# Products of zeros on TensorE, in a two-block transformer on one Trainium2 core

## The reference

```python
h = x * rsqrt(mean(x**2, -1) + eps) * norm_g * (1 + scale) + shift   # second block
x = x + 0.5 * gate[0] * swiglu(h, w_in, w_out)                       # feed-forward
x = x + gate[1] * mixer(adaln(x))
```

## Time and profile before

| | |
|---|---|
| median of 3 runs | 3921.24 us (3918.16 to 3923.84) |
| profiled execution | 3914.14 us, span 3912.5 us |
| mean granted clock of TensorE | 0.905 of 2.4 GHz |
| TensorE busy (matmul) | 3438.6 us, 88% of the span |
| VectorE busy | 2347.7 us, 60% |
| ScalarE busy | 1507.4 us, 39% |

### The profile page before, as it was taken

The page is one execution under the profiler, slowest core; times in us unless marked ns, Lnnn a source line. Parts: engine busy times, 40 slices in busy tenths (PEclk is TensorE's granted clock), DMA queues, the critical chain, the costliest instruction groups (busy, mean ns, idle before and its releaser), DMA issues. The chain is left out here.

```text
span 3912.5 us, 68263 instructions
## 1 busy us (share of the span) xinstructions
PE 3438.6 (88%) x28885; PEld 3248.8 (83%) x28885; DVE 2347.7 (60%) x3355; ACT 1507.4 (39%) x2038; POOL 155.0 (4%) x148
## 2 busy tenths in 40 slices
PE   6688999999985788999997499999599999859799
PEld 5578999999983778999995499999389998648599
DVE  5547886456764436767676557676657646354454
ACT  3314444434452114444462244444454444311243
POOL 0001111110000100000000000000000000001000
PEclk9769999998997888999996699999799999878799
DMA  8326885445831004768541047685037444200142
GB/s 338 130 119 245 314 311 228 182 187 225 313 135 54 2 2 180 299 235 310 213 172 46 1 186 297 231 310 202 35 153 297 188 185 159 77 21 2 75 175 84
DMA packets 74781, 676.76 MB, mean 173 GB/s; under 512 B 8480, under 2 KB 12608, under 8 KB 52160
## 3 DMA queue, kind: packets, MB, share of 16 engines
q1 hardware_dynamic: 30400, 509.96, 33.6%
q10 hardware_dynamic: 41472, 151.01, 10.1%
q0 software_dynamic: 2688, 12.59, 1.2%
HBM read 669.29 MB, written 4.23 MB: 172 GB/s over the span
## 5 line engine op out<-in xcount | busy, mean ns | idle before, releaser
L1109 DVE TENSOR_TENSOR w_split<-ring,w_split 128x1024 fp32r<-128x1024 f32 x705 | 873.5, 1242 | 603.5 <-ACT w_split L1004 601.1
L1004 ACT ACTIVATE w_split<-ring 128x1024 fp32r<-128x1024 f32 x705 | 742.8, 1057 | 1077.2 <-PE banks L934 853.5
L932 PE MATMUL banks<-u_split,w_split 128*128 128x256 f32 x3840 | 1093.1, 285 | 13.9 <-DVE w_split L1109 7.3
L933 PE MATMUL banks<-u_split,w_split 128*128 128x256 f32 x3840 | 1090.1, 284 | 0.0
L934 PE MATMUL banks<-u_split,w_split 128*128 128x256 f32 x3840 | 1089.9, 284 | 0.0
L932 PEld LDWEIGHTS banks<-u_split,w_split 128*128 128x128 f32 x3840 | 741.5, 193 | 19.8 <-DVE w_split L1109 16.2
L933 PEld LDWEIGHTS banks<-u_split,w_split 128*128 128x128 f32 x3840 | 741.2, 193 | 0.5
L934 PEld LDWEIGHTS banks<-u_split,w_split 128*128 128x128 f32 x3840 | 740.7, 193 | 0.0
L932 PE MATMUL banks<-h_split,w_split 128*128 128x256 f32 x1920 | 543.6, 283 | 2.9 <-DVE w_split L1109 2.9
L933 PE MATMUL banks<-h_split,w_split 128*128 128x256 f32 x1920 | 543.4, 283 | 0.0
L934 PE MATMUL banks<-h_split,w_split 128*128 128x256 f32 x1920 | 543.3, 283 | 0.0
(11 more groups left out here) (395 smaller groups left out, 3986.8 us busy)
## 6 DMA issues: line engine op xcount, KB each, us to landing
ring<-stream SPq DMA_DIRECT2D x147, 3072.0 KB, 10.8
bufs<-ada ACTq DMA_DIRECT2D x288, 512.0 KB, 10.9
bufs<-ada SPq DMA_DIRECT2D x8, 2048.0 KB, 9.0
bufs<-ada POOLq DMA_DIRECT2D x8, 1024.0 KB, 7.6
bufs<-c_rows SPq DMA_DIRECT2D x8, 512.0 KB, 4.3
bufs<-gate_rows POOLq DMA_DIRECT2D x32, 128.0 KB, 8.0
ring<-stream SPq DMA_DIRECT2D x3, 1024.0 KB, 4.9
ring<-stream SPq DMA_DIRECT2D x1, 2816.0 KB, 10.4
```

Source lines behind the costliest of these rows:

```text
L932: pe.matmul(out, w(0), x(0), start=start, stop=False, skip_group_check=True)
L933: pe.matmul(out, w(0), x(1), start=False, stop=False, skip_group_check=True)
L1004: nc.scalar.activation(w_split[:, slot, 0, :], piece(j, b), ACT.Copy).then_inc(high.sem, 1)
L1109: e = nc.vector.tensor_tensor(w_split[:, slot, 1, :], piece(j, b), w_split[:, slot, 0, :].bitcast(F32), ALU.subtract)
```

## The change

`project_first_pair` does its product of zeros ten times instead of once. A new helper, `zero_products`, does `n` products of zeros of 256 columns that add to the right half of a PSUM bank which nobody reads then. `token_sums` gets a parameter `filled`: so many of these products ahead of each chunk's wait. Both kinds of `NextNorm` call it with 1. The root kind also does six of them ahead of the wait for the inverse root, and four behind the spread. The direct calls of `token_sums` in other stages keep `filled=0`.

```diff
@@ project_first_pair
-    pe.matmul(bank, core.zeros[:, 0:P], core.zeros[:], start=True, stop=True)
+    for _ in range(10):
+        pe.matmul(bank, core.zeros[:, 0:P], core.zeros[:], start=True, stop=True)
     pe.wait_ge(low.sem, low.at(2))
@@
+def zero_products(core, pe, bank, n):
+
+    for _ in range(n):
+        pe.matmul(core.psum[:, bank, SEQ:2 * SEQ], core.zeros[:, 0:P], core.zeros[:, 0:SEQ], start=False, stop=True, skip_group_check=True)
+
+
-def token_sums(core, pe, rows, bank, arrived, summed, n=KC, per=1, first=0):
+def token_sums(core, pe, rows, bank, arrived, summed, n=KC, per=1, first=0, filled=0):
     for c in range(first, first + n):
         if arrived and c % per == 0:
+            zero_products(core, pe, (bank + 2) % 8, filled)
             pe.wait_ge(arrived.sem, arrived.at(c // per + 1))
@@ NextNorm.on_tensor, kind "mean"
-            token_sums(core, pe, core.x, self.bank, self.ready, self.summed)
+            token_sums(core, pe, core.x, self.bank, self.ready, self.summed, filled=1)
@@ NextNorm.on_tensor, kind "root"
-            token_sums(core, pe, self.squares, self.bank, self.squared, self.summed)
+            token_sums(core, pe, self.squares, self.bank, self.squared, self.summed, filled=1)
+            zero_products(core, pe, (self.bank + 2) % 8, 6)
             pe.wait_ge(inverse.sem, inverse.at(self.turn + 1))
             spread_tokens(core, pe, 2, ROOT_BANK, self.spread)
+            zero_products(core, pe, (self.bank + 2) % 8, 4)
```

## The result

The changed kernel takes 3939.52 us (median of 5, 3936.33 to 3941.90), the kernel before 3921.24 beside it. The ratio is 1.0050, 95% interval 1.0039 to 1.0061: slower by 18.3 us, where +22.6 was forecast.

The account below looks back on a forecast made before the run. The prediction took TensorE to bound the kernel, in the norms' sums too. Norms +31.1 us less starts 8.5 made +22.6 on the median of 3921.2, so 3944 us; range 3930 to 3952, chance 0.57.

Parts of the forecast that it names:

- The bound of the norms: In the norms' sums TensorE never waits, so each of eight zero products costs its slot: 1.1 us per root norm.
- The 0.5 taken off for a warmer start: Twelfth root norm, before the first macaron stage: 3.0 us at half clock, less 0.5 for a warmer start behind it.
- The eleven: Root norms that follow a dense stage: 2.2 us more each, 24.2 in all.
- The slot of a zero product between one-column ones: In the norms' sums, a 256-column zero product costs 0.12 us at full clock, 0.21 at half; no row showed it.
- The six: Between a root norm's sums and spread: 0 at full clock, 0.45 us at half, taken as 0.3.
- The four: Behind a root norm's spread, with nothing to cover them: 0.48 to 0.85 us, taken as 0.8.
- The mean norms: Three norms: those at 240 and 260 at half clock, 1.7 us each, the one at 865 at full, 1.0; together 4.4.
- The clock falls as now: In the norms the fill is too thin to hold the clock, which falls as before, somewhat later in a few.
- the first rival: The fill holds the clock everywhere, with clock 1.0 throughout the sums: -14 us, 3907; chance 0.12.
- The starts: Ten zero products fill the waits before real products, and the feed-forward starts gain too: 8.5 us back in all.
- Gain 1.3 each, 3.9: Three output stages of 8 chunks: ten zeros fit the 4.61 us wait and real products then run at full clock.
- The signs: In norms: sums 4.6 to 5.5 us, gap near 0.7, next stage 0.5 to 0.9 later, spreads 0.5; output starts clock 1.0.

Follow-up runs that it names:

- e3: Changed kernel with only the eight zero products among the sums of the 15 norms, first pairs with one; 3929.79 us, ratio 1.0032 to the kernel before.
- e5: Changed kernel with only the six zero products ahead of the wait for the inverse root, first pairs with one; 3918.62 us, ratio 1.0002 to the kernel before.
- e4: Changed kernel with only the four zero products behind the spread of the 12 root norms, first pairs with one; 3927.74 us, ratio 1.0024 to the kernel before.
- e9: Changed kernel, norms filled, with the first pairs' zero products in two groups instead of ten in a row; 3931.72 us, ratio 1.0029 to the kernel before.
- e2: Changed kernel with only the fill of the norms, first pairs with one zero product as before; 3943.22 us, ratio 1.0060 to the kernel before.
- e6: Changed kernel with three zero products ahead of each chunk of the sums instead of one; 3949.75 us, ratio 1.0085 to the kernel before.
- e1: Changed kernel with only the ten zero products in front of the first pairs, norms as before; 3904.59 us, ratio 0.9963 to the kernel before.
- e12: The kernel of e1 run again on another day; 3904.23 us, ratio 0.9970 to the kernel before.
- e7: As e1, but the zero products are numbered by the wait they fill, 10 to 50 by stage; 3907.56 us, ratio 0.9974 to the kernel before.
- e8: As e1, but zero products in two groups, the second behind the wait for the first weight piece's low part; 3904.96 us, ratio 0.9965 to the kernel before.
- e10: As e8, but 40 and 8 zero products in the first projection and one in the wide time-mix stages; 3913.07 us, ratio 0.9976 to the kernel before.

## Why the prediction was right

- **The bound of the norms.** "TensorE never waits in the sums, so each costs its slot" holds: behind the dense stages the trace has no wait in the sums, and e3's norms are longer by what the slots cost. Predicted for the twelve root norms 24.2 + 3.0 = 27.2, measured in the profiled execution 24.6. The 0.5 taken off for a warmer start behind the twelfth didn't come: that stage's first products end after 11.9 us as before.
- **The eleven, part by part.** In the changed kernel's trace the sums are 11.5 us longer in all (eight each, forecast 12.1), the gaps to the spread 4.2 (the six, 3.3), the stretches behind the spread 7.9 (the four, 8.8), and the spreads 1.5 shorter (nothing). That is 22.1 for 24.2.
- **The slot of a zero product between one-column ones.** No row had it; taken as 0.12 and 0.21, measured 0.11 and 0.20.
- **The six** were put at 0.3 each, between 0 and 0.45; the delay is 0 or 0.60. The term of the half clock, 0.45, was 0.15 short, and in e5 it doesn't show in the time.
- **The four** were put at 0.8; 0.45 at full clock and 0.83 at half (0.77 and 1.15 behind the spread against 0.32). e4 costs 8.4 us, for 12 x 0.8 = 9.6.
- **The mean norms** were put at +4.4 and measured +1.6: the one at 260 cost 1.5 and the one at 865 2.1, but the one at 240 became 1.9 shorter. Two steps missed. One is that those at 240 and 260 run at half clock: in the changed kernel's execution the one at 240 had full clock for most of its sums. The other is that the one at 865 runs at full clock and costs 1.0: its clock fell while the sums ran (0.79 in their stretch).
- **The clock falls as now.** It fell in six of eleven norms during the sums (six or seven in e9 and e2), and the first rival's condition, clock 1.0 in the sums throughout, came true only with three zero products per chunk. Its price for the eleven norms, 15.8 less 5.5 and 4.2, was for one per chunk. With the three that held the clock, the eleven cost 26.6 us more than before in e6: the fill costs more slots than the clock gives back.
- **The starts** were put at 7.7 us for the pairs and 0.8 for the feed-forward stages, measured 4.8 and 2.2. The term that failed is "Gain 1.3 each, 3.9" for three output stages: two gave 1.26, the window attention's gave 0.02. I took it that the ten run at half clock there as elsewhere. They run at full clock in that stage. The earlier trace rows leave out its row, which tells it: the one zero product took 0.47 us, not 0.76, and the clock was at full when the stage began.

```profile
2844.58:2849.19 4.61, 0.47 (x2) 0.16 (x2) 3.88 (x6) 4.61 (x7) 0.00 (x0) 0.63 0.00 0
```

  The same happens behind the filled norms: the fill makes the ten shorter (2.5 us as recorded, for 3.6 to 4.6 in e1) and so undoes part of what they are for. The two projections gave 2.1 for the 3.0, and the mamba output -0.2 for the 0.5. The feed-forward stages gave more than forecast because their own zero products run faster behind the fill: in six of nine the first real product comes 0.5 us sooner (1.75 us after the start for 2.2 to 2.3), and in three of these the first 48 end sooner (after 8.1 us, for 8.5, 9.3 and 8.6).
- **The sum.** The four filled places hold +19.3 of the profiled +25.4; the rest lies in stages that no edit touches, such as the projection of the last time mix (40.2 and 43.0 us). The medians differ by 18.3. Part of the agreement is luck: by the medians the norms' fill alone costs 23.9 us (e2) and the ten alone give 13 to 15 (e1, e12), which would make +9 to +11. Only together do they make 18. The forecast of 8.5 for the starts fits the traces, not the time of the ten alone.
- **The signs.** Of the signs named for "right", the stretch behind the spread (0.45 to 0.83 us longer) came as said. The sums took 4.6 to 6.4 us, not at most 5.5. The gap to the spread stayed near 0.7 in only three of eleven norms. The clock was 0.5 in eight of eleven spreads, and the output stages' pairs had full clock in two of three.

## What to carry to other kernels

Work put on an engine to keep its clock up is free only where that engine waits; first look at who was last there, the engine or its operand. Where it is the engine, count slots: here the fill of 15 norms costs 24 us, and nine starts give 5 to 13 by the traces. Where it does wait, a number of fillers that fits at half clock ends early at full clock. To end shortly ahead of the real work at either, tie the last part to an event near the end of the wait, not to a count. In these traces that made the starts 5 to 8 us shorter than ten in a row do; the time of e7 and e8 isn't below e1's, so that this pays in the whole kernel is not shown.

## What the runs showed of the hardware

- Products of zeros count as work for the clock: behind 4.4 us of them the output stages' first real products run at full clock (1487.60 above), at half without them. In e1 and e7 the clock of one such stage rose only 1.4 and 1.3 us into them.
- With one 256-column product ahead of each four one-column ones the clock fell during the sums in six of eleven norms; with three it was 1.00 in all eleven of e6's.
- The idle time between the last zero product and the pair goes with the pair's clock. I counted the output stages, the mamba projection and the window projection in the nine traces with filled pairs. Where that idle was up to 1.5 us, the pair ran at 1.00 in 31 of 35 cases; where it was 2.1 to 3.5 us, the mean clock was 0.77 to 0.87 in all 17. The gap doesn't decide alone: the window attention's output stage had 0.55 us of it in e8, e9 and e10, and clocks of 1.00, 0.77 and 0.77.
- The kernel without the change runs from 3907 to 3929 us. Stages with no edit in them have two or three lengths by where the clock changes: the chunk stage of the first time mix 163.5, 168.4 or 169.5 us, the projection of the last one 39.1 to 45.8. A local account in the trace tells 1 us; the median of the time here does not tell 5 for certain.
